# One decoder layer on one core: the second prompt tile as a stream of its own, run between the expert slots of the samples and the first tile

## What is computed

```python
h = rmsnorm(x) @ w_in                      # split among four mixers
x = x + merge(rwkv7(h), fox(h), sgu(h), dilated(h)) @ w_out
x = x + cross_attend(rmsnorm(x), ca_wq, ca_wo, mk, mv)
x = x + peer_ffn(rmsnorm(x), peer_wq, keys, u_tab, v_tab)
y = rmsnorm(x)

def peer_ffn(...):                         # per token
    q = (xt @ wq).reshape(PEER_BLOCK, PEER_HEADS, 2, PEER_DK // 2)
    s = einsum('phcd,hcnd->phcn', q, keys)
    top_s, top_i = top_k(s, 16)            # of 128 keys, twice per head
    best_s, best_j = top_k(cand_s, 16)     # of the 16 x 16 sums
    act = gelu(einsum('pd,phkd->phk', xt, u_tab[e_idx]))
    return einsum('phk,phkd->pd', softmax(best_s) * act, v_tab[e_idx])
```

## Time and profile before

| | |
|---|---|
| time, median of three runs | 1295.68 us (1295.6 to 1297.0) |
| the profiled execution, in all | 1299.01 us |
| its span, first to last instruction | 1297.2 us |
| mean granted TensorE clock | 0.948 of full |
| PE, DVE, ACT, POOL busy | 85%, 51%, 34%, 29% of the span |
| DMA | 387.99 MB, 299 GB/s over the span |

### The profile page before, as it was taken

One profiled execution on the slowest core, in us unless ns is written; L12 is line 12 of the kernel. 1 busy time (PEld: TensorE's weight loads), 2 busy tenths in 40 slices (PEclk: granted clock), 3 DMA queues, 4 the chain that ended last, 5 costly groups with the idle time before them and its releaser, 6 DMA issues.

```text
span 1297.2 us, 12851 instructions
## 1 busy us (share of the span) xinstructions
PE 1100.2 (85%) x4406; PEld 604.8 (47%) x4406; DVE 658.9 (51%) x1685; ACT 446.5 (34%) x1249; POOL 380.4 (29%) x382
## 2 busy tenths in 40 slices
PE   5999999796888997989999987788777877877776
PEld 4777877564566765644444432232222322322211
DVE  2361222455311222456576666767666666667554
ACT  3232210333202212144443444434544344444343
POOL 0410012550000000124444455344443443434430
PEclk9999996897988998989999999999999999999989
DMA  9431131842164863489999999999999999999995
GB/s 306 131 99 33 33 118 58 285 150 78 45 244 153 353 242 98 141 329 416 387 428 415 401 410 427 427 427 426 426 426 427 427 426 427 426 427 427 426 427 213
DMA packets 96642, 387.99 MB, mean 299 GB/s; under 512 B 8320, under 2 KB 53312, under 8 KB 57152
## 3 DMA queue, kind: packets, MB, share of 16 engines
q0 software_dynamic: 43520, 306.24, 56.9%
q1 hardware_dynamic: 50752, 78.83, 17.5%
q10 hardware_dynamic: 2304, 2.10, 0.5%
HBM read 381.19 MB, written 5.42 MB: 298 GB/s over the span
## 4 chain that ended last, share of the span: by engine, by line
PE 53%; DMA 29%; ACT 9%; DVE 5%; POOL 2%; issue 2%; ACTq 0%; SPq 0%; POOLq 0%; DVEq 0%
DMA near<-peer_uv,idx 19%; PE ps L1106 15%; PE ps L606 14%; PE ps L614 9%; DMA far<-peer_uv,idx 8%; PE ps L714 1%; ACT L1389 1%; ACT L1400 1%; ACT dg L1409 1%; DVE near L1953 1%; PE ps L1088 1%; ACT wv L1404 1%; PE ps L985 1%; PE ps L610 1%; PE ps L1026 1%
## 5 line engine op out<-in xcount | busy, mean ns | idle before, releaser
L1106 PE MATMUL ps<-near,dg 128*128 128x512 f32 (+1 forms) x852 | 419.2, 622 | 80.2 <-ACT dg L1409 80.2
L2043 POOL DMA_INDIRECT near<-peer_uv,idx x213 | 232.6, 1092 | 404.5 <-PE ps L1106 286.0
L1953 DVE CUSTOM_DVE_ANT_0 near<-near,XN 128x1024 f32<-128x1024 f32 x192 | 235.3, 1225 | 154.3 <-DMA near<-peer_uv,idx 153.9
L1106 PEld LDWEIGHTS ps<-near,dg 128*128 128x128 f32 (+1 forms) x852 | 149.9, 187 | 313.3 <-ACT dg L1409 179.6
L1106 PE MATMUL ps<-far,dg 128*128 128x512 f32 (+1 forms) x300 | 148.7, 625 | 44.3 <-ACT dg L1409 44.3
L606 PE MATMUL ps<-xT,W 128*128 128x288 f32 x672 | 182.8, 416 | 1.3 <-DVE xT L1452 0.9
L1400 ACT ACTIVATE gl<-act 128x1 f32<-128x1 f32 x288 | 57.9, 201 | 326.0 <-DVE act L1953 325.7
L606 PEld LDWEIGHTS ps<-xT,W 128*128 128x128 f32 x672 | 129.5, 195 | 64.1 <-issue 34.6
L1409 ACT ACTIVATE dg<-const,wv 128x128 f32<-128x128 f32 (+1 forms) x288 | 113.0, 393 | 19.3 <-PE ps L1106 10.3
L1106 PEld LDWEIGHTS ps<-far,dg 128*128 128x128 f32 (+1 forms) x300 | 48.8, 179 | 142.9 <-ACT dg L1409 98.0
L2043 POOL DMA_INDIRECT far<-peer_uv,idx x75 | 78.7, 1049 | 109.8 <-PE ps L1106 101.7
(11 more groups left out here) (393 smaller groups left out, 1131.3 us busy)
## 6 DMA issues: line engine op xcount, KB each, us to landing
W<-w_in SPq DMA_DIRECT2D x11, 1024.0 KB, 5.5
MR<-mk_s SPq DMA_DIRECT2D x8, 1024.0 KB, 14.0
MR<-mv_s SPq DMA_DIRECT2D x8, 1024.0 KB, 10.6
W<-peer_wq SPq DMA_DIRECT2D x8, 1024.0 KB, 5.5
W<-ca_wk SPq DMA_DIRECT2D x4, 1024.0 KB, 5.7
W<-ca_wv SPq DMA_DIRECT2D x4, 1024.0 KB, 5.6
W<-w_out SPq DMA_DIRECT2D x4, 1024.0 KB, 6.6
W<-ca_wq SPq DMA_DIRECT2D x4, 1024.0 KB, 5.3
```

The lines of the kernel that those rows point to most:

```text
L1106: ins = mm(PS[0:m, 2 + 2 * t + half, :], dg[:, n % DGS, 0:m], row(n)[:, D + half * 512:D + (half + 1) * 512], start=False, stop=False, ski ...
L1953: V.tensor_tensor_reduce(out=u, in0=u, in1=x, scale=1.0, scalar=0.0, op0=ALU.mult, op1=ALU.add, accum_out=M["act"][:, par, k:k + 1]).then_ ...
L2043: G.indirect_dma_start(row(n), None, io["peer_uv"], bass.IndirectOffsetOnAxis(ap=M["idx3"][:, it % 3, k:k + 1], axis=0))\
```

## The change

The columns are put in the order samples, first tile, second tile. The first 160 columns (phase "A") go through all stages alone, in a list `FIRST` like the old one. The list `THEN` comes after: the last four blocks of peer_wq for phase A, and then all stages for the second tile (phase "B") with 28 blocks of w_in, w_out, ca_wq, ca_wo and peer_wq loaded a second time. Loads in phase B use two places for weights, since a sixth row buffer (`w2`) takes the third. `THEN` is cut into 90 pieces, and 58 pairs of expert slots are spread evenly over the cuts; on each engine a pair stands in program order between two pieces of the dense work. PE lags one pair. The other 86 pairs follow, with the final pass of each tile hooked in between. Row buffers: five, six from slot 10 on, thirteen from slot 124 on.

The experts are done in nine groups of 32 tokens, 32 slots each, with four heads side by side in the 128 rows of a slot; the diagonal matrix is 128 x 32 for all slots, and PE adds the four strips in one bank. ACT copies the sum of each group away, to DRAM for the first five; the normed tokens of a group are loaded back from DRAM in four copies (`XR`), and the residual and the groups are added at the end.

```diff
-TILES = [(0, P), (P, P), (T, TS)]
+NA = TS + P
+TILES = [(TS, P), (NA, P), (0, TS)]
...
+BLOCKS = W_IN + MEMORY + TAIL + W_IN + TAIL
+SECOND = 40
...
+        s = b % RING if b < SECOND else (b - SECOND) % 2
...
-NEAR, FAR = 8, 5
-WIDE = 6 * TOPK
+GROUPS = [0, 0, 0, 0, 2, 1, 1, 1, 1]
+PER = 32
+NEAR, FAR = 5, 7
+WIDE = 124
...
+    THEN = (
+        [("lin", P_A + 4 + i) for i in range(4)] + [("score", ("A", 1)), ("first", 1), ("norm_b", None)]
+        + [("lin", IN_B + i) for i in range(4)]
+        + [("rw_pre", "B"), ("rw_kk", "B"), ("lin", IN_B + 4), ("rw_vec", "B"), ("rw_tile", 1), ("rw_scan", "B"),
+           ("rw_out", "B")]
+        + [("lin", IN_B + i) for i in range(5, 12)] + [("lf", "B")]
+        + [("attn", (1, s)) for s in range(11)]
+        + [("sgu", "B"), ("gnorm", ("B", (0, 2))), ("gnorm", ("B", (1, 3)))]
+        + [("lin", OUT_B + i) for i in range(4)] + [("norm", (0, "B"))] + [("lin", Q_B + i) for i in range(4)]
+        + [("cross", (1, s)) for s in range(7)]
+        + [("lin", O_B + i) for i in range(4)] + [("norm", (1, "B"))]
+        + [("lin", P_B + i) for i in range(4)] + [("score", ("B", 0))]
+        + [("lin", P_B + 4 + i) for i in range(4)] + [("score", ("B", 1))])
+    CUTS = {"rw_pre": 2, "rw_kk": 2, "rw_tile": 10, "rw_scan": 3, "rw_out": 2}
+    EARLY = 58
...
+    def pairs_at(c):
+        return range(c * EARLY // NCUTS, (c + 1) * EARLY // NCUTS)
...
+        def slot_pair():
+            n = 2 * done[0]
+            g = n // PER
+            pe.wait_ge(*at("act_dg", n + 1))
+            if n % PER == 0 and g:
+                pe.wait_ge(*at("act_fs", g - 1))
+            for x in (n, n + 1):
+                for half in range(2):
+                    rows = slice(64 * half + 32 * (x % 2), 64 * half + 32 * (x % 2) + 32)
+                    ins = mm(PS[rows, ACC, :], dg[:, x % DGS, :], row(x)[:, D + half * 512:D + (half + 1) * 512],
+                             start=x % PER < 2, stop=x % PER >= PER - 2, skip_group_check=True)
+                ins.then_inc(*inc("pe_v", x))
+            done[0] += 1
...
+        def load_xr(g):
+            if g >= 2:
+                sp.wait_ge(*at("dve_u", PER * (g - 1) - 1))
```

More of the change, by code:

```diff
@@ L259, in sbuf_map @@
     put("U0n", GW)
-    put("YLT", 2, N)
-    put("Y0", 2, N)
+    put("YLT", 2, NA)
+    put("Y0", 2, NA)
+    put("NP", 8, 2, HD)
     put("MT", 8, 2, P)
-    put("NP", 8, 2, HD)
-    put("ST", 9, 2, HD)
+    near = places["MT"] + 4 * 4 * 2 * P
+    put("shift", KC, B)
     put("S0T", B, 2, HD)
@@ L330, in sbuf_map @@
     put("ef", 2, TOPK)
[L331 to L337, removed]
-    put("far", FAR, 2 * D)
[L339 to L344, removed]
+    assert at[0] <= places["cols"]
+    at[0] = places["W"] + 2 * 4 * KC * WCOLS
+    put("w2", 2 * D)
+    assert at[0] <= places["stat"]
+    at[0] = base
+    put("far", FAR, 2 * D)
+    assert at[0] <= near, (at[0], near)
+    at[0] = late
+    put("FS", 4, 512)
+    put("X1f", 2, D)
+    put("gF", D)
+    assert at[0] <= base
     return m
@@ L384, in program @@
     rT, kT, vT = hT[:, 0:2, :], hT[:, 2:4, :], hT[:, 4:6, :]
[L388 to L395, removed]
     X1, XN, gr, hX, QX, MK, MV, MR, SCx, PTx, SSx, PTy, softx = (
         M[k] for k in ("X1", "XN", "gr", "hX", "QX", "MK", "MV", "MR", "SCx", "PTx", "SSx", "PTy", "softx"))
[L398 to L425, removed]
+    keys, SA, dg, XR, FS, X1f, gF = (M[k] for k in ("keys", "SA", "dg", "XR", "FS", "X1f", "gF"))
     SC, PT, LFU, lf, soft = (M[k] for k in ("SC", "PT", "LFU", "lf", "soft"))
@@ new lines, in scaled_of, with follow @@
+    def scaled_of(i):
+        return M["xn1"][:] if i == 4 else M["xn"][:, i % 2, :]
+    def follow(stages, between, pair):
+        for name, argument in FIRST:
+            if name in stages:
+                steps = stages[name](*(() if argument is None else (argument,)))
+                if steps is not None:
+                    for label in steps:
+                        between(label)
+        c = 0
+        for name, argument in THEN:
+            n = CUTS.get(name, 0)
+            if name in stages:
+                steps = stages[name](*(() if argument is None else (argument,)))
+                if steps is not None:
+                    for _ in steps:
+                        for p in pairs_at(c):
+                            pair(p)
+                        c, n = c + 1, n - 1
+                    assert n == 0, (name, n)
+            for _ in range(n + 1):
+                for p in pairs_at(c):
+                    pair(p)
+                c += 1
+        assert c == NCUTS
+        for p in range(EARLY, PAIRS):
+            pair(p)
+            if p in HOOKS and HOOKS[p][0] in stages:
+                stages[HOOKS[p][0]](HOOKS[p][1])
+        stages["end"]()
@@ new lines, in end @@
+        def end():
+            slot_pair()
+            pe.wait_ge(*at("act_fs", 8))
+            add_group(1, 3, 3).then_inc(*inc("pe_fin", 1))
+        pe.wait_ge(*at("dve_xT", 3))
+        follow({
+            "lin": linear, "mem_turn": lambda: turn(2, 4), "norm_b": lambda: turn(4, 5), "fill": fill, "rw_pre": rw_pre,
+            "rw_kk": rw_kk, "rw_vec": rw_vec, "rw_tile": rw_tile, "rw_scan": rw_scan, "rw_sample": rw_sample,
+            "rw_out": rw_out, "attn": attn, "sgu": sgu, "sattn": sattn, "gnorm": gnorm, "norm": norm, "cross": cross,
+            "scross_k": scross_k, "scross_v": scross_v, "score": score, "fin_sum": fin_sum, "fin_early": fin_early,
+            "end": end}, lambda label: gap(*label), pair)
@@ L1951, in rounds, with pair @@
+        later = [iter(())]
+        def pair(p):
+            for n in (2 * p, 2 * p + 1):
+                it, k = divmod(n, TOPK)
+                g, par = n // PER, it % 2
+                if k == 0 and it:
+                    for _ in later[0]:
+                        pass
+                    later[0] = topk(it + 2) if it + 2 < NIT else iter(())
+                if n % PER == 0:
+                    dve.wait_ge(S.sem(f"xr{g % 2}_in"), 64 * (g // 2 + 1))
                 dve.wait_ge(S.sem(f"row{PLACE[n]}_in"), LANDINGS[n])
```

1892 lines of the change are left out of this document (1099 added, 793 removed).

## The result

The change makes the kernel 8.7% slower: 1407.4 us (median of four runs, 1402.9 to 1412.0) against 1295.6, ratio 1.087 with the interval 1.082 to 1.092. The forecast was 1284. The profiled execution is the fastest of the four: it took 1402.9 us, and its span is 1400.8.

A forecast was written before the change was run, and what follows sets the result against it. It took dense stages, then gathers at the DMA engines' rate, then a tail as the bound. 414 + 435 + 437 = 1286 us of span, corrected by +1.8 and -3.3 to 1284; range 1246 to 1352.

The forecast's parts named there:

- The first gather: End of the first 160 columns' stages: savings sum to 128.7 us, so gathers start at 414 us, not 543.
- The other stages with their pairs: Second tile's stages outside the 32 blocks: 168 us alone, plus 35 pairs at 2.4 us each, 84 us.
- the rival of pairs in series: Pairs between stages cost DVE and ACT in turn, 4.1 us each, 144 instead of 84; 1344 us; 27%.
- its point of 2.7 us: Price of a pair between stages from which the pairs-in-series rival decides the outcome.
- The blocks: Second tile's 32 weight blocks with 23 pairs: PE needs 4.2 us each, transfers 6.0; 174 us taken.
- "18 us": Deduction for up to two weight blocks found loaded after other stages, seven stretches; bounds 0 and 34 us.
- the term for the clock: Second tile's stretch: PE idles more, so five slow starts after waits add 9 us.
- the half-clock rival: All 32 blocks run at half clock, 8.5 us each against 5.4: +98 us, 1382; half of them, 1333; 11%.
- the floor: DMA minimum for the second tile's stretch: 116 slots, 28 blocks and some 16 MB else, 394 us.
- a new wait: Second tile's stretch: gathers wait for PE to free rows, and late weight blocks make PE wait; no time added.
- After the stretch: Remaining slots: 166 gathers 408 us, copies and final pass 18, tail 11; 437 us.

The follow-up runs named there:

- pairs_off_blocks: The change with its 58 pairs placed only at the 58 cuts that are not a weight block, the 32 blocks in rows without slots; 1422.1 us.
- both_eighth: The change with second-stream weight blocks loading one eighth of their rows and gathers of the first 116 slots moving 1 KB rows, not 8 KB; 1291.9 us.
- w_long_rows: The change with all weight blocks laid out in DRAM in 8 KB pieces in place of eight of 1 KB; 1382.9 us.
- w_eighth: The change with each weight block of the second stream loading only one eighth of its rows; 1332.6 us.
- g_eighth: The change with gathers of the first 116 slots moving rows of 1 KB in place of 8 KB; 1323.9 us.
- late_memory_loads: The change with memory keys and values, gain rows, the rest and score keys loaded after the second stream's w_out blocks and first ca_wq block; 1401.5 us.
- long_three_late: The change with 8 KB weight pieces, three weight places with five row buffers until slot 124, and the late memory loads together; 1373.6 us.

## Why the prediction was wrong

**The first gather** was right: 409.3 for 414. The single terms of its sum were not measured apart.

**The other stages with their pairs** were right in size: 168 + 84 and some clock, against 246 us, and 228 with the transfers cut. If the stages alone take the 168 that was summed, 78 us are left for some 34 pairs, 2.3 each, so the rival of pairs in series and its point of 2.7 us were not met. No run took the pairs away, so the 168 is not shown. In pairs_off_blocks ten more pairs in the stages cost 47 us, so the price of a pair is not fixed.

**The blocks** are the step that failed: 192 us of transfers less "18 us" for weights that are already loaded, 174 in all and 183 with the term for the clock, where 280 were measured, 8.0 us a block. Three parts of it, by the runs:
- The count was low: 35 blocks stand after the first gather, where 32 were priced. The three of phase A end 17 us after it.
- The engines alone need 188 for the blocks (both_eighth), not 32 x 4.2 = 134. Besides some 16 us for the three blocks, PE's timeline of that run gives some 128 us of products for the other 32, where 32 x 3.59 = 115 were priced, 36 for 22 pairs of slots with their waits, where 21 were priced, and 7 for weights. A block that starts at the lower clock is slower. Of the w_out blocks, 32 products took 9.02 us at a granted clock of 0.79 after PE had waited 17.7 us, and 32 like them 7.58 at 0.94 in ca_wo, behind other products:

```profile
758.30 9.02 PE L858 MATMUL ps<-W,YT 128*128 128x256 f32 x32 [17.73 <-DMA W<-w_out]
832.89 7.58 PE L858 MATMUL ps<-W,YT 128*128 128x256 f32 x32
```

  Granted clock was 0.70 to 0.80 in the four block windows, where above 0.9 was expected. All products of the blocks took 160 us in the change; at the pace of the fastest of each form (3.84, 3.72 and 4.6 us a block) they would take some 135, an estimate. So the clock cost about 25 us, where 9 were priced: the half-clock rival was right in kind, and a quarter of its 98.
- The rest, 93 us, is transfers: PE's waits for weights are 80 us against 7 with the transfers cut, and the products 160 against 142, at a granted clock of 0.74 in the stretch (window from 409 to 937) against 0.80. I let the DMA engines run full through the blocks at 426.5 GB/s. Over the stretch they ran at 373 when busy (166.7 MB in 84.7% of 528 us), which alone lifts the floor from 394 to 447, and were busy 85%, because a late block, the pair behind it and that pair's gathers wait for each other. The prediction named this chain as a new wait and priced it at nothing.

**After the stretch** 464.9 in place of 437. The queue row from 937 to 1390 shows 180.2 MB of gathers, six slots more than the 166 counted:

```profile
q0 software_dynamic: 24743, 180.16, 95.7%
```

Of the 288 gathers 171 were issued after 937 us, so one slot was on its way at the end of the stretch, where six were counted: 15 us. All 186.7 MB of this window moved at 412 GB/s; at 426.5 they are 438 us and not 453, and at the 421 that the earlier trace rows showed for the whole expert stage they are 443. That the rest of the slower rate comes from copies of tokens and groups among the gathers is an inference: GB/s dips where such copies run, but no run took them away.

The range ended at 1352 because no rival priced the waits between the two streams, and the time after the stretch had no range. The miss is 92 us of stretch and 28 after it, less 5 before. That the first gather and the stages came out near their sums may in part be luck, since their terms were not measured apart.

On the clock the Trainium skill's page "TensorE: Matmul & The Clock Gate", Part 1, which calls the low clock the default that activity releases, fits the trace: a granted clock of 0.53, close to the lower level (1.2 GHz), in the window from 937 to 1390 us, where PE is busy 39%, against 0.98, close to the higher (2.4 GHz), at 79% in the earlier trace rows. No time hangs on it there, since the DMA share is 1.00.

## What to carry to other kernels

When a second stream is threaded between gathers on engines that run in program order, the price has two parts: the work that it adds to the engines (here 415 us with the transfers cut, which uses up the gain of the early start) and the waits that the two streams hand each other (here 111 us more). Price the engines and the transfers of the merged stretch apart, then ask how much is in flight when one of them is late; with few buffers the two overlap only in part (here DMA was busy 85% and PE 64%). A run with the transfers of the merged stretch left out tells whether tuning the overlap can pay at all. When a remedy trades one buffer for another, run each half of the trade: here a third weight place gained 37 us and the row buffer that paid for it cost 21.

## What the runs showed of the hardware

- Gathers of 8 KB rows held back weights in 1 KB pieces: from 614 to 619 us 1.80 MB of gathers moved and 0.27 MB of weights; with weights in 8 KB pieces, at the same place, 1.08 and 1.05 (w_long_rows).
- Of their own busy time, gathers moved at 389 GB/s in the stretch, and at 376 with the weights cut (w_eighth), so the weights beside them are not what slows them; after the stretch they moved at 415. Plain loads moved at 335 in 1 KB pieces, 323 with the gathers cut (g_eighth), and at 381 in 8 KB pieces. Why gathers are slower in the stretch than after it is open.
- A block with gathers on their way landed after them, those issued up to 2.5 us behind it too: 13.8 us at 607.69 and 14.7 at 632.04, against a median of 5.5 us for the blocks of the kernel before.
- Cutting one wait moved part of it: of 17.7 us at w_out 8.8 came back at ca_wq (late_memory_loads). With 1.4 us of waits for weights left in place of 80 (long_three_late), blocks were 78 us shorter and stages 41 longer.
